# Sums of gate weight blocks in a delta-rule stage: sixteen VectorE operations replaced by adding transfers

## What is computed

```python
h = _gdn_mixer(x, gdn_w_in[j], gdn_conv_w[j], gdn_a_log[j], gdn_dt_bias[j],
               gdn_norm_w[j], gdn_w_out[j])
...
# inside the mixer, in short: one projection gives q, k, v, z and the decay gates;
# q, k, v pass a convolution and the delta rule, head by head;
# out = norm(o) * silu(z), then the out projection
```

## Time and profile before

| what | us |
|---|---|
| median of 3 runs | 1011.79 (1010.11 to 1012.02) |
| the profiled execution | 1009.76 |
| span of its trace, first to last instruction | 1008.5 |
| mean granted TensorE clock, of full | 0.986 |
| TensorE busy | 962.1 |
| VectorE busy | 555.9 |
| ScalarE busy | 335.5 |
| GpSimd busy | 52.6 |
| mean DMA rate | 210 GB/s |

### The profile page before, as it was taken

The page is one execution under the profiler, slowest core; times in us unless marked ns, Lnnn a source line. Parts: engine busy times, 40 slices in busy tenths (PEclk is TensorE's granted clock), DMA queues, the critical chain, the costliest instruction groups (busy, mean ns, idle before and its releaser), DMA issues.

```text
span 1008.5 us, 21949 instructions
## 1 busy us (share of the span) xinstructions
PE 962.1 (95%) x9305; PEld 749.7 (74%) x9305; DVE 555.9 (55%) x1192; ACT 335.5 (33%) x904; POOL 52.6 (5%) x81
## 2 busy tenths in 40 slices
PE   9999999999999999799877899999999999999999
PEld 6788888888887794345322589988888988777887
DVE  3976876876878243111100586875555465194675
ACT  3456557556645121001000323132111321233550
POOL 1111011011010000000000000000000000034000
PEclk9999999999999999999987999999999999999999
DMA  9214224144156999999999934452555344652221
GB/s 348 87 65 153 81 71 183 45 148 169 45 203 271 423 374 352 420 432 428 432 429 413 413 144 154 164 181 92 183 181 187 117 168 167 190 188 84 84 84 43
DMA packets 33623, 211.63 MB, mean 210 GB/s; under 512 B 4384, under 2 KB 8928, under 8 KB 15088
## 3 DMA queue, kind: packets, MB, share of 16 engines
q1 hardware_dynamic: 33520, 210.16, 54.2%
HBM read 209.03 MB, written 1.11 MB: 208 GB/s over the span
## 4 chain that ended last, share of the span: by engine, by line
PE 81%; DMA 6%; SPq 5%; DVE 4%; ACT 2%; issue 2%; POOL 0%; DVEq 0%; ACTq 0%; POOLq 0%
PE ps L559 11%; PE ps L3164 9%; PE ps L3064 5%; PE ps L585 5%; SPq L1914 4%; DMA xt<-in_wu 4%; PE ps L3836 3%; PE ps L2910 3%; PE ps L2028 3%; PE ps L3805 3%; PE ps L3934 2%; PE ps L971 2%; PE ps L2673 2%; PE ps L3204 2%; PE ps L807 2%
## 5 line engine op out<-in xcount | busy, mean ns | idle before, releaser
L559 PE MATMUL ps<-xt,slots 128*128 128x256 f32 x512 | 122.3, 384 | 0.0
L559 PEld LDWEIGHTS ps<-xt,slots 128*128 128x128 f32 x512 | 93.8, 190 | 12.8 <-issue 0.4
L1306 DVE SCALAR_TENSOR_TENSOR arena<-arena 128x256 f32<-128x256 f32 x128 | 56.5, 500 | 0.0
L2028 PE MATMUL ps<-arena 128*32 128x512 f32 x224 | 47.0, 631 | 7.1 <-DMA arena<-in_w 6.1
L2368 DVE TENSOR_TENSOR arena<-arena,ps 128x256 f32<-128x256 f32 x8 | 3.4, 421 | 88.5 <-ACT arena L2158 88.5
L2028 PE MATMUL ps<-slots,arena 128*32 128x512 f32 x192 | 47.3, 638 | 2.8 <-DMA xt<-in_wu 2.8
L4337 POOL TENSOR_TENSOR arena<-arena 128x512 f32<-128x512 f32 (+1 forms) x8 | 17.8, 2260 | 597.6 <-DVE arena L4145 597.6
L2158 ACT ACTIVATE arena<-ps 128x256 f32<-128x256 f32 x8 | 3.1, 385 | 111.5 <-PE ps L2028 111.5
L971 PE MATMUL ps<-slots,yt 128*128 128x256 f32 x128 | 30.3, 396 | 2.1 <-DMA slots<-in_wu 2.1
L2028 PEld LDWEIGHTS ps<-arena 128*32 128x32 f32 x224 | 11.9, 115 | 26.5 <-issue 19.4
L3836 PE MATMUL ps<-xt,slots 128*128 128x256 f32 x128 | 30.6, 385 | 0.6 <-ACT arena L4037 0.6
(11 more groups left out here) (590 smaller groups left out, 2175.6 us busy)
## 6 DMA issues: line engine op xcount, KB each, us to landing
slots<-in_wu SPq DMA_DIRECT2D x91, 1024.0 KB, 5.6
arena<-in_wu SPq DMA_DIRECT2D x20, 1024.0 KB, 13.5
arena<-in_w SPq DMA_DIRECT2D x5, 4096.0 KB, 28.5
slots<-in_w SPq DMA_DIRECT2D x8, 2048.0 KB, 33.5
extra<-in_w SPq DMA_DIRECT2D x2, 4096.0 KB, 29.2
yt<-in_w SPq DMA_DIRECT2D x3, 2048.0 KB, 30.0
extra<-in_wu SPq DMA_DIRECT2D x4, 1024.0 KB, 19.6
xt<-in_wu SPq DMA_DIRECT2D x4, 1024.0 KB, 30.6
```

The source lines that it names most:

```text
L559: q = M.matmul(bank(b, T), self.slots[:, s, k, n * P:(n + 1) * P], self.xt[:, k, :], start=(k == 0), stop=(k == KT - 1))
L1306: q = V.scalar_tensor_tensor(g.cn[:, s], src, w, g.cn[:, s], ALU.mult, ALU.add)
L2028: q = M.matmul(self.ps[r, 2, :], g.xg[:, half * (KT // 2) + k, r], self.flat(slots[e])[:, k * 512:(k + 1) * 512], start=(half == 0 and k = ...
```

## The change

The 16 operations of `mix_z` go away. In their place GpSimd issues transfers from the weights in HBM: a plain one lays a block into the target tile, and one with `accum_op=ALU.add` adds a block to what is there. Since only adding is done so, the sums have other signs and terms: t1 = b11 + b12, t2 = b11 + b12 + b22, t4 = b11 + b12 + b22 + b21, and in slot 4 b12 + b22. The row sums and folds on VectorE get other signs to match. Per pair there are ten transfers of 512 KB: three plain ones (t1, t2 and t4 each begin as b11) and seven adding ones. Those into one target must follow one another, so GpSimd waits for the earlier ones to land before it issues the next.

`first_sums(p, n)` makes t1 and t2, `last_sums(p, n)` the sum in slot 4 and t4. For pair 0 they stand around and between compact_rest, the masks and copy_x of head 0. For a later pair first_sums stands in the odd head before the pair, and last_sums begins there and goes on in the pair's even head. TensorE's waits are set to the new signals.

```diff
             elif m == 1:
                 M.wait_ge(*g.z_rows_made(4))
-                M.wait_ge(*g.z_mix(4 * p + 2))
+                M.wait_ge(*g.first_sums(5 * (p + 1)))
             elif m == 2:
-                M.wait_ge(*g.z_mix(4 * p + 3))
+                M.wait_ge(*g.last_sums(5 * p + 3))
             elif m == 5:
-                M.wait_ge(*g.z_mix(4 * p + 4))
+                M.wait_ge(*g.last_sums(5 * (p + 1)))
...
-            V.tensor_tensor(rows[:, 0], y21, y22, ALU.add).then_inc(*g.z_rows_made.up())
+            V.tensor_tensor(rows[:, 0], y21, y22, ALU.subtract).then_inc(*g.z_rows_made.up())
...
-                V.tensor_tensor(two[1], g.zu3, src, ALU.add).then_inc(*g.z_folds.up())
-                V.tensor_tensor(two[0], g.zu2, src, ALU.add).then_inc(*g.z_folds.up())
+                V.tensor_tensor(two[1], src, g.zu3, ALU.subtract).then_inc(*g.z_folds.up())
+                V.tensor_tensor(two[0], src, g.zu2, ALU.subtract).then_inc(*g.z_folds.up())
...
-            if even:
-                mix_z(p, 0)
             turn_f(h, 2)
...
+        def weights_of(p):
+            one, two = (self.ins["wu"][U_GDN + 6 * p + u] for u in (2, 5))
+            return [u[:, n:n + HK, :] for u in (one, two) for n in (0, HK)]
+
+        def first_sums(p, n):
+
+            b11, b21, b12, b22 = weights_of(p)
+            t1, t2, t4 = g.z_mixes
+            if n == 0:
+                if p > 0:
+                    G.wait_ge(*g.z_products(5 * p - 1))
+                G.dma_start(t2, b11).then_inc(*g.first_sums.up())
+                G.dma_start(t1, b11).then_inc(*g.first_sums.up())
+            elif n == 1:
+                G.wait_ge(*g.first_sums(5 * p + 2))
+                G.dma_start(t2, b12, accum_op=ALU.add).then_inc(*g.first_sums.up())
+                G.dma_start(t1, b12, accum_op=ALU.add).then_inc(*g.first_sums.up())
+            else:
+                G.wait_ge(*g.first_sums(5 * p + 4))
+                G.dma_start(t2, b22, accum_op=ALU.add).then_inc(*g.first_sums.up())
+
+        def last_sums(p, n):
+
+            b11, b21, b12, b22 = weights_of(p)
+            t1, t2, t4 = g.z_mixes
+            if n == 0:
+                if p > 0:
+                    G.wait_ge(*self.multiplied[2](p))
+                G.dma_start(t4, b11).then_inc(*g.last_sums.up())
+            elif n == 1:
+                G.wait_ge(*g.last_sums(5 * p + 1))
+                G.wait_ge(*self.arrived[4](p + 1))
+                G.dma_start(self.slots[:, 4, 0:HK], b22, accum_op=ALU.add).then_inc(*g.last_sums.up())
+                G.dma_start(t4, b12, accum_op=ALU.add).then_inc(*g.last_sums.up())
+            elif n == 2:
+                G.wait_ge(*g.last_sums(5 * p + 3))
+                G.dma_start(t4, b22, accum_op=ALU.add).then_inc(*g.last_sums.up())
+            else:
+                G.wait_ge(*g.last_sums(5 * p + 4))
+                G.dma_start(t4, b21, accum_op=ALU.add).then_inc(*g.last_sums.up())
...
         G.wait_ge(*g.gate_kept(1))
+        first_sums(0, 0)
         compact_rest(0)
+        first_sums(0, 1)
         for h in range(QKH):
-            for l in range(1, 3):
-                mask(h, l)
+            p, ahead = h // 2, h + 1 < QKH
+            mask(h, 1)
+            if h == 0:
+                first_sums(0, 2)
+                last_sums(0, 0)
+            elif h % 2 and ahead:
+                first_sums(p + 1, 0)
+            mask(h, 2)
+            if h % 2 == 0:
+                last_sums(p, 1)
+            elif ahead:
+                first_sums(p + 1, 1)
             copy_x(h)
-            if h + 1 < QKH:
+            if h % 2 == 0:
+                last_sums(p, 2)
+            elif ahead:
+                first_sums(p + 1, 2)
+            if ahead:
                 compact_rest(h + 1)
+            if h % 2 == 0:
+                last_sums(p, 3)
+            elif ahead:
+                last_sums(p + 1, 0)
```

More of the change, by code:

```diff
@@ L435, in gdn @@
         g.taps = (g.tap_qk, g.tap_v)
-        g.z_rows_made, g.z_mix, g.z_folds = (new("DVE", n) for n in ("z_rows_mixed", "z_weights_mixed", "z_folded"))
+        g.z_rows_made, g.z_mix, g.z_folds = (new("DVE", n) for n in ("z_rows_mixed", "out_weights_mixed", "z_folded"))
+        g.first_sums, g.last_sums = (new("POOL", n, 16) for n in ("z_weights_t1_t2_summed", "z_weights_t3_t4_summed"))
         g.compact, g.compact_rest = new("ACT", "blocks_compact"), new("POOL", "blocks_compact_rest")
@@ L452, in gdn @@
         gate_pairs = QKH // 2
-        g.out_mixed = lambda q, n: g.z_mix(4 * gate_pairs + 4 * q + n)
+        g.out_mixed = lambda q, n: g.z_mix(4 * q + n)
         g.out_rows_made = lambda n: g.z_rows_made(4 + n)
@@ L1436, in mix_z_rows @@
             V.wait_ge(*g.z_rows_made(3))
[L1437 to L1455, removed]
+            V.tensor_tensor(rows[:, 3], y12, rows[:, 1], ALU.add).then_inc(*g.z_rows_made.up())
         def fold_z(p, m):
@@ L1637, in gdn_vector @@
             conv(h, 1, 0)
-            if even:
-                mix_z(p, 1)
             if not ahead:
@@ L1644, in gdn_vector @@
             conv(h, 1, 1)
-            if even:
-                mix_z(p, 2)
             if not ahead:
@@ L1677, in gdn_vector @@
                     fold_out(0, n)
-            if even:
-                mix_z(p, 3)
             if ahead:
@@ L1706, in gdn_gpsimd @@
         G = self.nc.gpsimd
+        HK = KT // 2
         by_cc = lambda a: a.rearrange("p a b i -> p a (b i)")
```

## The result

The changed kernel took 1035.32 us (median of 5 runs, 1028.56 to 1037.05) beside 1011.33 us of the kernel before (1008.93 to 1012.02): ratio 1.0235, interval 1.0218 to 1.0253. It is slower by 24 us; the forecast was 1017.8 us, with a range to 1024. The profiled execution is the one of 1028.56 us, the lowest of the five, with a span of 1027.3 us against 1008.5: the traces show 18.8 us of the loss.

A forecast was written before the change was run, and what follows sets the result against it. The prediction took the order of TensorE's work as the bound, TensorE being full from 46 to 291 us. A 4.1 us stall plus 1.9 us of low clock gave +6.0 us on 1011.79, so 1017.8 us; range 1010 to 1024 us.

The forecast's parts named there:

- The place: Pair 0's third gate product in the delta-rule stage: TensorE stalls 4.1 us there, from 47.52 to 51.60 us.
- round 3: Pair 0's adds into slots[4] and t4, issued from 44.05 us and landing at 51.60 us.
- the direction: The whole kernel gets slower, by 6.0 us; chance of slower 0.59.
- the price of an issue: GpSimd's time to issue one transfer, taken as 0.92 us, its mean for the mask.
- the rival of dear issuing: On GpSimd, an issue above 3.08 us delays every head's first mask; at 4 us, 1027 us or more; chance 0.07.
- The trail of low clock: On TensorE after the stall at pair 0's third product, matmuls at lower clock lose another 1.9 us.
- a round with more than one transfer: At pair 0, two adding transfers land 7.55 us after first issue: 5.1 us plus 2.45 us for the second.
- The upper bound: At pair 0, crowded transfers take 8.8 us each time, landing last at 56.6 us: +11 us, 1022.8 us.
- the step had it end at 40.44: In head 0, mask(0,2) on GpSimd ends at 40.44 us, in time for TensorE, which wants it at 40.39 plus 0.5.
- 0 for the seven later heads: Pairs 1 to 3: transfers stay hidden, masks come in time and added traffic delays no weights; cost 0.
- Nothing changes: At pair 0, adding transfers land like plain ones, 5.1 us each time, before the third product: 1011 to 1013 us; chance 0.35.
- Faster: The whole kernel gains more than 2 us, to at the most 1009.5 us; chance 0.06.

The follow-up runs named there:

- Experiment 3: The changed kernel with the adding left out, all 40 transfers being plain copies: 1018.59 us, ratio 1.0091 to the kernel before.
- experiment 1: The changed kernel with pair 0's sums made by VectorE again, pairs 1 to 3 still by transfers: 1017.7 us, ratio 1.006 to the kernel before.
- experiment 8: The kernel before with VectorE's bars(1) of head 0 moved behind the sum t2: ratio 1.0008 to the kernel before.
- experiments 4: The changed kernel with pair 0's transfers issued from about 5 us on, ahead of compact_rest(0): 1033.25 us, ratio 1.0224 to the kernel before.
- experiment 12: The changed kernel with pair 0's t4 copy and slot 4 add issued with its first transfers: 1026.78 us, ratio 1.0179 to the kernel before.
- experiment 2: The changed kernel with pair 0's sums by transfers, pairs 1 to 3 by VectorE's additions: 1027.97 us, ratio 1.017 to the kernel before.

## Why the prediction was wrong

**What was right.** The place: line 586 waits for a transfer of round 3, at pair 0 and nowhere else (the add into t4, whose count the wait takes in, not the one into slots). That this wait reads 3.8 us where 4.1 were forecast is chance: TensorE came to it late, after 2.2 us of waits for masks, pauses of 0.8 and 4.1 us and a slow second product, all of which lie under the same rounds. Right too were the direction, that VectorE's 17 us are worth nothing, and the price of an issue, taken as 0.92 us: GpSimd's groups by line give 0.57 to 0.64 us for a plain one and 0.86 to 1.23 us for an adding one,

```profile
L1722 POOL DMA_DIRECT2D arena<-in_wu x4 | 4.9, 1228 | 0.0
...
L1721 POOL DMA_DIRECT2D arena<-in_wu x4 | 3.6, 900 | 10.8 <-DMA arena<-in_wu 10.8
...
L1734 POOL DMA_DIRECT2D arena<-in_wu x4 | 2.6, 642 | 0.0
```

so the rival of dear issuing fell: no mask after head 0 is waited for. A single adding transfer in quiet, priced at 5.1 us, landed after 5.5 us (the one of line 1742 at 137 us). The trail of low clock, 1.9 us, measured 1.4.

**The term that was mis-sized: a round with more than one transfer.** Three rounds were to take 7.55 + 6.3 + 7.55 = 21.4 us; they took 10.9 + 10.6 + 8.3 = 29.8 us, from the first issue of each to its last landing. The prediction let the second transfer of a round cost its bytes at the rate of a full queue, 2.45 us. Experiment 3 shows that two plain ones take 6.5 to 7.8 us, 1.4 to 2.7 us over the 1 MB row I used; three such rounds took 21.4 us, the very sum that was given to the adding ones. By the prediction's prices that sum is 15.3 us for plain rounds and 6.1 for the adding; measured were 21.4 and 8.4, so the greater part of the error, 6.1 of 8.4 us, is in two transfers at once and not in the adding. Two 512 KB transfers on GpSimd's queue were priced by one of 1 MB on SyncE's, and that row is not of the same thing. The upper bound, 8.8 us a round, was too low too. I had called the crowded row an upper end for a quiet machine, without asking whether the rounds themselves would make the crowd; the share was 0.69 from 50 to 60 us. With the mask of line 1755 ending at 44.15 us (43.08 + 1.07), where the step had it end at 40.44, the third product came 13.7 us late instead of 4.1.

**The step that failed: "0 for the seven later heads".** Its first half, GpSimd's queue, held. Its second half read an average: the queues would stay "about two thirds full". They did, 0.66 of the time from 75 to 320 us; but the windows around the pauses are full:

```profile
156.00:162.00 6.00, 5.68 (x96) 4.82 (x90) 3.98 (x10) 2.32 (x7) 1.85 (x2) 1.00 1.04 296
...
237.00:243.00 6.00, 4.72 (x174) 3.59 (x173) 3.78 (x13) 0.77 (x2) 0.00 (x0) 1.00 0.99 215
```

And it asked only which weights could be late. The page of before lists every user of the DMA engines, and a queue named "instruction" is among them; I did not ask who waits for that one. TensorE does, once in 256 instructions. By the medians the later pairs cost 6.7 us (experiment 1).

**The rivals.** *Nothing changes* had as its point of decision 5.8 us a round; even plain copies missed it (experiment 3), so it fell on the term above. The Trainium skill's formula (DMA: Bandwidth & Descriptors, Anatomy of one DMA), by which a round of 1 MB takes 4.4 us, leads to the same rival; measured were 6.5 to 7.8 us for plain rounds, and the measurement decides. *Faster* fell with experiment 8.

**Had I taken** 10 us for each round, the sum of the prediction's own steps would have put round 3's landing at 30.18 + 30 = 60.2 us, the stall at 12.7 us and the time at 1011.79 + 12.7 + 1.9 = 1026.4 us. With the 6.7 us of the later pairs that is 1033 us, near the 1035.3 measured.

**What stays open.** Why 2 KB rows spare TensorE, whether it is the length of a row or how many rows stand queued on one DMA engine; and why GpSimd at times does not issue. Such a stop came behind adding transfers: between the two adds of every pair with 2 KB rows, and with 4 KB rows only in experiments 4 and 12. All 18 of them end 0.2 to 0.4 us after an adding transfer issued earlier has landed, so it is a landing that GpSimd stands for; why only there, no run shows. Nor is a pause always due to GpSimd's transfers: in experiment 2 there is one of 0.80 us at 207 us, at row 6594, where only SyncE's fills are on their way. A free moment of the DMA engines when the instructions are due seems to be what counts, and where these moments fall shifts with every edit.

## What to carry to other kernels

Moving work from an idle engine's spare time to the DMA engines is no gain when the engine was off the path, and the DMA engines carry more than the weights: look at every queue of the page, the one of instructions too, and at the share in the stretch of a burst, not its mean. Transfers that must follow one another cost their landing time each, and a row for one transfer is no price for two in flight. So count the rounds in series before the first reader; if one round can be taken out of the series, as in experiment 12, that is worth more than starting earlier on a queue with other duties.

## What the runs showed of the hardware that was not expected

- An adding transfer of 512 KB takes 1.9 times the engine time of a plain one (46.9 against 24.7 us, summed over the engines). Alone it lands after 5.5 us, or after 8.6 to 9.4 us beside SyncE's fills (line 1725 from 100 us on); a round with one beside another transfer took 8.3 to 10.9 us at pair 0.
- TensorE pauses of 0.2 to 4.1 us, with no semaphore behind them, in the middle of matmul groups; all 47 of thirteen kernels stand at steps of 256 of TensorE's instructions and end 2.2 to 2.5 us after the start of a 16 KB packet of the instruction queue. A pause of 1.72 us cost 3.5 us, through the clock.
- GpSimd stood up to 9.3 us between two issues of adding transfers without a wait in the program, until 0.2 to 0.4 us after an earlier one had landed.
